# Attention stages and branch stage of a two-block fp32 layer: later output transposes, projection matmuls between transposes, and the first gates' tile moved into the last attention head

## The chip, the cores and the metric

One Trainium2 chip, one core of it. The metric is the device time of one execution in microseconds (us), the median of several runs.

## The reference, cut to what matters

Input is x of 1024 positions by 1024 channels, fp32. The first block normalises x and projects it; three branches follow (a gated linear recurrence, a differential attention of 4 heads of 2 x 64, a forgetting attention of 8 heads of 64), which are mixed by gates:

```python
h = rmsnorm(x, norm1_g); proj = h @ w_in            # q, k, v, gates, ...
o_diff = diff_attention(dq, dk, dv, lam, rel_bias)  # softmax(c=0) - lam * softmax(c=1), times v
y_diff = rmsnorm(o_diff, diff_subln_g) * (1 - lam_init)
y_fox = forgetting_attention(fq, fk, fv, log_f)
g = sigmoid(gates + gate_b)                         # three gates of 1024
m = g[0] * (y_rnn @ w_br_rnn) + g[1] * (y_diff @ w_br_diff) + g[2] * (y_fox @ w_br_fox)
x = x + m @ w_out
```

A feed-forward layer and a second block (SSD, HGRN2 and S5 mixers) follow; the change does not touch them.

## The kernel before, in words

Every fp32 matrix product is made of three fp32r matmuls: each operand is split into a high and a low part, and high x high, high x low, low x high are added in PSUM. The activations' parts are AH and AL (`act_high`, `act_low`). A weight tile of 128 columns goes through WeightTiles (line 75): SP loads it to `raw`, ACT copies it to `high` (split_high, L138), POOL makes `low` (split_low, L145), PE multiplies (multiply, L163). There are two slots; the semaphores raw_free, loaded, high, low and used count turns per slot. A whole tile is 8 x 3 x 2 = 48 matmuls of 128x512; a tile of w_br_diff or w_br_fox (NK = 4) is 24. Slots may be filled by the stage before through `Ahead` ("ready"): its tiles are split before the stage ends.

**stage_attention** runs twice, as "diff" and then as "fox". A head has 8 steps, in the order of query blocks 0, 7, 1, 6, 2, 5, 3, 4; h is the head, i the place in that order, j = 8h + i. In the program's order PE does in step j: scores(j+2) (L1332), matmuls of the projection of a later head into the bank pP (project_ahead, L1315), values(j) (L1364 for diff, L1368 for fox), more of the projection, and turned(j+1): transposes of the probabilities into the banks pT[0] and pT[1] in turn (L1351), in groups of up to four. A group may start when ACT or DVE has evacuated the group two before it. With fox both sides c = 0, 1 are transposed, so a block of 5 or more has four groups; with diff it has two. `projecting(j)` says which piece of the projection belongs to step j: 12 matmuls a step for the heads to come. In diff the last ten steps project the first head of fox (`follow`); in fox nothing is left to project there. ACT does in step j: exps(j+2), take_high(j) (fox), a take of a finished projection, evacuate(j+1), weight splits at i = 3 and i = 7. DVE does combine(j+1), reduce(j+2), take(j), evacuate(j+1).

In diff the outputs of a head must be normalised and transposed: ACT's out_root at i = 7, DVE's scale_out (L1610) writes o_scaled at i = 0 of the next head, PE's turn_out (L1377) transposes it into pT[0] and pT[1] in the same step, ACT's out_high and DVE's out_low (L1615) take it. The next transposes into these banks wait for out_low ("yl").

**stage_mix_branches** begins with the two attended branches. For each of eight chunks n and for j = 0 (diff), 1 (fox): PE multiplies the gate's tile (slot 0, 48 matmuls, pG[j]) and the branch's half tile (slot 1, 24 matmuls, pY[j]); ACT writes gate[j] = sigmoid(pG[j] + gate_b) (L625); DVE multiplies it by pY[j] (L739), adds the two (L741), and SP stores the sum. The first tile of each slot is made ahead by fox. Then follow the recurrent branch (8 pairs of whole tiles, from turn RNN_AT of the slots), its gates and its product, and w_out. SP loads the first attended tiles, then four `taps` and four `bias` rows of 4-byte elements (L445, L447), two gate tiles of the recurrence, and goes on in a loop. `over_loop` is a hardware loop with its last round written out. Each stage ends with a barrier.

Of the kernel before, what the change touches and what calls it, by code (L numbers as in the profile page):

```python
# [78 lines left out]
class WeightTiles:  # L79
# [7 lines left out]
    def __init__(self, core, ctx, sem, nk, width=P, name="w", slots=2, ready=True, place=None):  # L87
        self.sem, self.nk, self.width, self.name, self.slots = sem, nk, width, name, slots
        self.ready = ready if isinstance(ready, tuple) else (ready,) * slots
# [33 lines left out]
    def load(self, sp, slot, turn, src, nk=None):  # L123

        nk = nk or self.nk
        if self.given(slot, turn):
            return
# [4 lines left out]
    def split_high(self, act, slot, turn, nk=None):  # L132
# [3 lines left out]
        act.wait_ge(self.s("loaded", slot), (turn + (1 - self.ready[slot])) * 16)  # L136
# [192 lines left out]
def stage_mix_branches(core, X, ahead):  # L329
# [20 lines left out]
    RNN_AT = 2 * KD  # L350
# [11 lines left out]
    with stage(core) as (ctx, sem):  # L362
        W = WeightTiles(core, ctx, sem, KD)
        WR = WeightTiles(core, ctx, sem, G, HALF)
        A_next = Ahead(core, sem, ahead)
        gate_b = sbuf(core, ctx, "gate_b", [P, 3, KD])
        gate = [sbuf(core, ctx, f"gate{j}", [P, SEQ]) for j in two]
        other = [sbuf(core, ctx, f"other{j}", [P, SEQ]) for j in two]
# [33 lines left out]
        with nc.Block() as block:  # L402

            @block.sync
            def _(sp):
# [3 lines left out]
                def load_attended(n):  # L409
                    for j, (g, w, _) in enumerate(attended):  # L410
                        W.load(sp, 0, n * 2 + j, w_in[:, bass.ds(n * P + GATES_AT + g * D, P)])
                        W.load(sp, 1, n * 2 + j, w[:, bass.ds(n * P, P)], NK)

                def store(n):
                    sp.wait_ge(sem("sum"), n + 1)
                    sp.sem_inc(sem("store_asked"), 1)
                    sp.dma_start(m_tile(n), gate[0][:, :]).then_inc(sem("m_stored"), 16)
# [25 lines left out]
                load_attended(0)  # L443
# [5 lines left out]
                with sp.Fori(1, KD) as n:  # L449
                    load_attended(n)  # L450
                    store(n - 1)
# [5 lines left out]
                sp.wait_ge(sem("m_stored"), KD * 16)  # L457
# [21 lines left out]
            def _(pool):  # L479
                W.open_pool(pool)  # L480

                def attended_low(n):
                    for j in two:
                        W.split_low(pool, 0, n * 2 + j)
                        W.split_low(pool, 1, n * 2 + j, NK)
# [5 lines left out]
                first_then_loop(pool, KD, attended_low)  # L491
# [15 lines left out]
            def _(pe):  # L507
                W.open_pe(pe)
                pe.sem_inc(sem("gates_free"), 1)
                with pe.Fori(0, KD) as n:  # L510
                    for j, (_, _, y0) in enumerate(attended):
                        W.wait(pe, 0, n * 2 + j)
                        pe.wait_ge(sem(f"pg_free{j}"), n + 1)
                        W.multiply(pe, 0, pG[j], AH, AL)
                        W.wait(pe, 1, n * 2 + j)
                        pe.wait_ge(sem(f"py_free{j}"), n + 1)
                        W.multiply(pe, 1, pY[j], YH[:, y0:y0 + NK, :], YL[:, y0:y0 + NK, :], NK)

                def rnn(n, first):
                    W.wait(pe, 0, n + RNN_AT)  # L520
                    if first:
                        pe.wait_ge(sem("pg_free0"), KD + 1)
# [4 lines left out]
                    if first:  # L527
                        pe.wait_ge(sem("pg_free1"), KD + 1)
# [88 lines left out]
            def _(act):  # L617
                for j in two:
                    act.sem_inc(sem(f"pg_free{j}"), 1)  # L619
                act.wait_ge(sem("gate_b"), 48)  # L620

                def sigmoid_attended(n, j):
                    act.wait_ge(W.s("used", 0), n * 2 + j + 2)
                    act.wait_ge(sem(f"gate_free{j}"), n + 1)
                    act.activation(gate[j][:, :], flat2(pG[j]), ACT.Sigmoid, bias=gate_b[:, attended[j][0], bass.ds(n, 1)]).then_inc(sem(f"pg_free{j}"), 1)  # L625

                def attended_turn(n, more):
                    for j in two:
                        turn = n * 2 + j + 1
                        W.split_high(act, 0, turn if more or j == 0 else RNN_AT)  # L630
                        sigmoid_attended(n, j)
                        if more or j == 0:
                            W.split_high(act, 1, turn, NK)
                        else:
                            W.split_high(act, 1, RNN_AT)
# [3733 lines left out]
```

## Time and profile before

| what | us |
|---|---|
| three runs | 3072.69, 3068.14, 3072.55 |
| median | 3072.55 |
| the profiled execution, own time | 3067.96 |
| its span, first to last instruction | 3066.2 |
| diff attention, first to last matmul | 90.5 to 311 |
| fox attention, first value matmul to last value matmul | 313.2 to 568.1 |
| branch stage's first matmul | 570.4 |

Times in the rows are microseconds from the span's start. A row of the timeline gives start, duration, engine, line, operation, what it writes from what it reads, shape and count; in brackets the idle time of that engine just before, and what ended it. PE is TensorE's matmuls, DVE VectorE, ACT ScalarE, POOL GpSimd, SP the engine that issues most transfers. "issue" means that the profile shows nothing waited for. PEclk is the granted clock as a share of full speed.

### The profile page before, as it was taken

The page shows a single profiled execution, that of the slowest core. Times are in us where ns is not written, and L with a number is a line of the kernel's source. Part 1 is how long each engine was busy: PE and PEld are TensorE (multiplying, and loading weights), DVE is VectorE, ACT ScalarE, POOL GpSimd, SP SyncE. Part 2 cuts the span into 40 slices and gives each one's busy share as a digit, 9 for nine tenths or more (in the row PEclk, how much of TensorE's full clock was granted, in tenths as well). Part 3 has the DMA queues.
Part 4 walks back from the last instruction along what each step waited for, and adds up shares of the span by engine and source line. Part 5 has one row for each costly group of instructions (what it writes and reads, how often), then busy time and mean ns, then how long its engine had stood idle before and what let it go on. Part 6 is the DMA issues. An engine that isn't in the chain of part 4 may idle for free. (4 is left out here: it accounts for less than half of the span.)

```text
span 3066.2 us, 38258 instructions
## 1 busy us (share of the span) xinstructions
PE 2947.0 (96%) x14910; PEld 2389.5 (78%) x14910; DVE 1413.7 (46%) x2142; ACT 1147.5 (37%) x1587; POOL 735.0 (24%) x396
## 2 busy tenths in 40 slices
PE   8999999899999999999999999989999999999988
PEld 6777766688877788878888888877777888878776
DVE  4466244211155413344343444375553566555776
ACT  3355244322266512322222222253442554325443
POOL 2110100022211222221124421112232333123552
PEclk9999999999999999999999999999999999899988
DMA  4110200221211123131112111125323111323343
GB/s 141 44 42 8 76 28 25 41 65 56 78 47 46 53 80 117 49 88 41 41 48 62 48 48 41 41 90 103 72 87 103 42 28 35 110 43 112 119 150 110
DMA packets 250129, 203.69 MB, mean 66 GB/s; under 512 B 38453, under 2 KB 219141, under 8 KB 249997
## 3 DMA queue, kind: packets, MB, share of 16 engines
q1 hardware_dynamic: 247820, 200.84, 22.5%
q8 instruction: 88, 1.44, 0.2%
q10 hardware_dynamic: 2176, 1.05, 0.2%
q14 instruction: 45, 0.36, 0.0%
HBM read 174.69 MB, written 27.16 MB: 66 GB/s over the span
## 5 line engine op out<-in xcount | busy, mean ns | idle before, releaser
L145 POOL TENSOR_TENSOR w_low<-w_raw,w_high 128x1024 fp32r<-128x1024 f32 (+1 forms) x181 | 418.7, 2313 | 1704.8 <-ACT w_high L138 1701.5
L138 ACT ACTIVATE w_high<-w_raw 128x1024 fp32r<-128x1024 f32 (+1 forms) x181 | 180.9, 1000 | 417.1 <-PE mix_banks L163 292.0
L163 PE MATMUL ffn_banks<-act_high,w_high 128*128 128x512 f32 x688 | 268.8, 391 | 4.0 <-POOLq L112 4.0
L163 PE MATMUL ffn_banks<-act_high,w_low 128*128 128x512 f32 x688 | 268.4, 390 | 0.0
L163 PE MATMUL ffn_banks<-act_low,w_high 128*128 128x512 f32 x688 | 268.4, 390 | 0.0
L163 PE MATMUL mix_banks<-act_high,w_high 128*128 128x512 f32 x640 | 252.3, 394 | 2.3 <-POOLq L112 2.3
L163 PE MATMUL mix_banks<-act_high,w_low 128*128 128x512 f32 x640 | 249.1, 389 | 0.0
L163 PE MATMUL mix_banks<-act_low,w_high 128*128 128x512 f32 x640 | 249.0, 389 | 0.0
L163 PEld LDWEIGHTS ffn_banks<-act_high,w_high 128*128 128x128 f32 x688 | 129.7, 189 | 31.2 <-POOLq L112 4.3
L2063 DVE TENSOR_TENSOR x<-x,ffn_banks 128x512 f32<-128x512 f32 x176 | 117.8, 685 | 73.9 <-PE ffn_banks L1829 73.4
L163 PEld LDWEIGHTS ffn_banks<-act_high,w_low 128*128 128x128 f32 x688 | 129.6, 188 | 27.0
L163 PEld LDWEIGHTS ffn_banks<-act_low,w_high 128*128 128x128 f32 x688 | 129.6, 188 | 26.9
L1829 PE MATMUL ffn_banks<-v_high,f_high 128*128 128x512 f32 x352 | 140.8, 400 | 9.6 <-DVE x L2063 9.4
L1948 ACT ACTIVATE u_val<-ffn_banks,conv 128x1024 f32<-128x1024 f32 x21 | 25.3, 1207 | 321.4 <-PE ffn_banks L163 321.4
L163 PEld LDWEIGHTS mix_banks<-act_high,w_high 128*128 128x128 f32 x640 | 120.1, 188 | 29.0 <-ACTq L619 2.5
L163 PEld LDWEIGHTS mix_banks<-act_low,w_high 128*128 128x128 f32 x640 | 120.1, 188 | 26.7 <-issue 1.9
L163 PEld LDWEIGHTS mix_banks<-act_high,w_low 128*128 128x128 f32 x640 | 120.1, 188 | 25.0
L1829 PE MATMUL ffn_banks<-v_high,f_low 128*128 128x512 f32 x352 | 139.4, 396 | 0.0
L1829 PE MATMUL ffn_banks<-v_low,f_high 128*128 128x512 f32 x352 | 137.7, 391 | 0.0
L1442 ACT ACTIVATE scores<-scores,low 128x1024 f32<-128x1024 f32 (+7 forms) x128 | 98.4, 770 | 100.7 <-DVE low L1552 100.6
L739 DVE TENSOR_TENSOR gate<-gate,mix_banks 128x1024 f32<-128x1024 f32 x16 | 19.5, 1221 | 231.3 <-PE mix_banks L163 231.3
L2071 DVE SCALAR_TENSOR_TENSOR u_val<-ffn_banks,conv,u_val 128x1023 f32<-128x1023 f32 x21 | 26.9, 1283 | 198.5 <-ACT u_val L1948 198.5
(660 smaller groups left out, 7000.6 us busy)
## 6 DMA issues: line engine op xcount, KB each, us to landing
w_raw<-in_w_in SPq DMA_DIRECT2D x106, 512.0 KB, 4.1
w_raw<-in_ffn_up SPq DMA_DIRECT2D x44, 512.0 KB, 3.9
w_raw<-in_w_out SPq DMA_DIRECT2D x24, 512.0 KB, 3.8
v_raw<-in_ffn_down SPq DMA_DIRECT2D x11, 1024.0 KB, 5.1
decay<-acum_rows SPq DMA_DIRECT2D x16, 512.0 KB, 3.7
exp_c<-exp_acum_rows SPq DMA_DIRECT2D x16, 512.0 KB, 5.2
x_ring<-in_x SPq DMA_DIRECT2D x8, 512.0 KB, 9.8
m_part<-gate SPq DMA_DIRECT2D x8, 512.0 KB
```

Source lines behind the costliest of these rows:

```text
L138: act.activation(self.high[slot][:, 0:nk, :], self.raw[slot][:, 0:nk, :], ACT.Copy).then_inc(self.s("high", slot), 1)
L145: pool.tensor_tensor(self.low[slot][:, 0:nk, :], self.raw[slot][:, 0:nk, :], self.high[slot][:, 0:nk, :].bitcast(F32), ALU.subtract).then_ ...
L163: last = pe.matmul(out[:, h, :] if not halves else out[h], w[slot][:, k, :], x[:, k, cols], start=(n == 0), stop=(n == 3 * nk - 1))
L739: dve.tensor_tensor(gate[j][:, :], gate[j][:, :], flat2(pY[j]), ALU.mult).then_inc(sem(f"py_free{j}"), 1)
L1442: act.activation(tile, tile, ACT.Exp, scale=-1.0, bias=low[:, b, c:c + 1], accum_out=total[:, b, c:c + 1]).then_inc(sem("probs"), 1)
L1829: last = pe.matmul(pD[:, bank_of(i, q), :], x[:, k, steps(b)], w[0][:, k, half * HALF:(half + 1) * HALF], start=(n == 0), stop=(n == 3 * G ...
L1948: act.activation(U[:, :], flat2(pU[slot]), ACT.Identity, scale=taps[:, 2, bass.ds(n, 1)], bias=bias[:, bass.ds(n, 1)]).then_inc(sem(f"tap2 ...
L2063: dve.tensor_tensor(X[:, b, cols], X[:, b, cols], pD[:, bank_of(i, q), :], ALU.add).then_inc(sem("added"), 1)
L2071: dve.scalar_tensor_tensor(out=U[:, 1:], in0=x[:, :SEQ - 1], scalar=taps[:, 1, bass.ds(n, 1)], in1=U[:, 1:], op0=ALU.mult, op1=ALU.add).th ...
```

## The change

Three parts. (1) In diff, turn_out, out_high and out_low move from step i = 0 to i = 1 of the next head, with the wait on "yl" and the split of the step's projection. (2) Where a step has projection matmuls left after values(j) and the next block has four groups of transposes, they are issued between its second and its third group. (3) Fox's last ten steps project two gate tiles (`follow` = the first tiles of gates 1 and 2) in pieces of 6 x 12 and 4 x 6 matmuls into first_q and first_k, which the branch stage takes as gate[0] and gate[1] and passes through a sigmoid in place. The branch stage's attended loop then runs half tile, gate tile of the next chunk, half tile, gate tile: all half tiles in slot 0 but the very last, gate tiles in slot 1; two gate tiles fewer. Slot 1 is handed over loaded but not split ("raw"). The sum goes to other[0]. SP's tap, bias and recurrence loads come ahead of the loop's.

```diff
 class WeightTiles / __init__
+        states = ready if isinstance(ready, tuple) else (ready,) * slots
+        self.ready = [state is True for state in states]
+        self.loaded = [state in (True, "raw") for state in states]
 stage_mix_branches
-    RNN_AT = 2 * KD
+    RNN_AT = 2 * KD - 1
+        W = WeightTiles(core, ctx, sem, KD, ready=(True, "raw"))
+        gate = [core.first_q, core.first_k]
 ... sync
+                def load_attended(n, more):
+                    W.load(sp, 0, n * 2 + 1, y_tile(n, 1), NK)
+                    W.load(sp, 1, n * 2 + 1, g_tile(n + 1, 1))
+                    W.load(sp, 0, n * 2 + 2, y_tile(n + 1, 0), NK)
+                    if more:
+                        W.load(sp, 1, n * 2 + 2, g_tile(n + 2, 0))
+                    else:
+                        W.load(sp, 1, n * 2 + 2, y_tile(n + 1, 1), NK)
-                load_attended(0)
                 for j in range(4):
                     sp.dma_start(taps[:, j, :], per_channel(io["rnn_conv_w"][0, j])).then_inc(sem("small"), 16)
...
+                def attended_turn(n, more):
+                    load_attended(n, more)
+                    store(n)
+                over_loop(sp, KD - 1, attended_turn)
 ... tensor
+                with pe.Fori(0, KD - 1) as n:
+                    for j in two:
+                        attended_y(n, j, 0, n * 2 + j)
+                        W.wait(pe, 1, n * 2 + j)
                         pe.wait_ge(sem(f"pg_free{j}"), n + 1)
-                        W.multiply(pe, 0, pG[j], AH, AL)
+                        W.multiply(pe, 1, pG[j], AH, AL)
+                for j in two:
+                    attended_y(KD - 1, j, j, 2 * KD - 2)
 ... scalar
+                def sigmoid_attended(n, j):
+                    act.wait_ge(W.s("used", 1), n * 2 + j)
+                    act.wait_ge(sem("sum"), n)
+                    act.activation(gate[j][:, :], flat2(pG[j]), ACT.Sigmoid, ...).then_inc(sem(f"pg_free{j}"), 1)
+                def attended_turn(n, more):
+                    W.split_high(act, 0, n * 2 + 1, NK)
+                    W.split_high(act, 1, n * 2 + 1)
+                    W.split_high(act, 0, n * 2 + 2, NK)
+                    sigmoid_attended(n + 1, 0)
+                    W.split_high(act, 1, n * 2 + 2, None if more else NK)
+                    sigmoid_attended(n + 1, 1)
+                W.split_high(act, 1, 0)
+                act.wait_ge(sem("gate_b"), 48)
                 for j in two:
+                    act.activation(gate[j][:, :], gate[j][:, :], ACT.Sigmoid, ...).then_inc(sem(f"pg_free{j}"), 1)
 ... vector
                     dve.wait_ge(sem("m_stored"), (n + 1) * 16)
+                    dve.tensor_tensor(other[0][:, :], gate[0][:, :], gate[1][:, :], ALU.add).then_inc(sem("sum"), 1)
 stage_attention
-    last_head = NH if diff else NH - 1
+    last_head = NH
+    last_counts = (12, 12, 12, 12, 8, 8, 8, 8, 8, 8) if diff else (12,) * 6 + (6,) * 4
 ... turned
+                    for at, (N, n, c, g, count) in enumerate(own_groups(j)):
+                        if between and at == 2:
+                            project_ahead(*between)
...
-                        if diff and i == 1 and h and n < ends[0, 0] + 2:
+                        if diff and h and ends[1, 0] <= n < ends[1, 0] + 2:
                             pe.wait_ge(sem("yl"), 2 * (h - 1) + n % 2 + 1)
 ... steps on PE
-                        before = 0 if j == last_step else 4 if i == 0 and h else 8
+                        before = 0 if diff and j == last_step else 4 if diff and i == 1 and h else min(8, count)
...
-                    if diff and i == 0 and h:
+                    if diff and i == 1 and h:
                         turn_out(h - 1)
-                    if ahead_now and count > before:
-                        project_ahead(H, g, first + before, count - before)
+                    rest = (H, g, first + before, count - before) if ahead_now and count > before else None
+                    inside = rest and j < last_step and len(own_groups(j + 1)) > 2
+                    if rest and not inside:
+                        project_ahead(*rest)
                     if j < last_step:
-                        turned(j + 1)
+                        turned(j + 1, rest if inside else None)
 first_block
+        stage_attention(core, "fox", FQ, FK, FV, 4, [(0, w_diff[:, 0:P]), (1, gate(1)[:, P:2 * P])], follow=(GATES_AT + D, GATES_AT + 2 * D))
```

ACT's out_high and DVE's out_low get the same condition `i == 1`. At its end fox's ACT waits until the raw tile has landed.

## Rows read from the trace of the kernel before

**Rows 1.** Page: busy time, share of the span and instructions of each engine.

```profile
PE 2947.0 (96%) x14910; PEld 2389.5 (78%) x14910; DVE 1413.7 (46%) x2142; ACT 1147.5 (37%) x1587; POOL 735.0 (24%) x396
```

**Rows 2.** Windows: busy (count) of PE, PEld, DVE, ACT, POOL; PEclk, DMA share, GB/s.

```profile
464.26:519.28 55.02, 53.18 (x378) 37.30 (x377) 26.00 (x88) 26.59 (x63) 4.79 (x2) 1.00 0.07 22
519.28:561.80 42.52, 32.16 (x281) 20.98 (x280) 25.19 (x84) 21.57 (x56) 1.39 (x1) 0.96 0.01 1
570.40:698.00 127.60, 127.58 (x563) 105.65 (x564) 14.21 (x10) 31.66 (x31) 26.83 (x15) 1.00 0.28 63
```

**Rows 3.** PE's waits, total, times, longest: two within diff, one over the span.

```profile
PE pt L1377 <- DVE o_scaled L1610: 6.3, 4, 1.9
PE pt L1351 <- DVE y_low L1615: 2.0, 2, 1.0
...
PE pt L1351 <- issue: 13.0, 16, 2.8
```

**Rows 4.** Timeline of PE in diff: three steps with output transposes.

```profile
167.53 0.70 PE L1332 MATMUL ps<-k,q 64*128 64x256 f32 x4
...
171.45 1.09 PE L1377 MATMUL pt<-ident,o_scaled 128*128 128x128 f32 x8 [1.86 <-DVE o_scaled L1610]
...
176.42 1.77 PE L1332 MATMUL ps<-k,q 64*128 64x512 f32 x8
...
216.78 0.70 PE L1332 MATMUL ps<-first_k,first_q 64*128 64x256 f32 x4
...
226.06 1.77 PE L1332 MATMUL ps<-first_k,first_q 64*128 64x512 f32 x8
...
309.11 1.09 PE L1377 MATMUL pt<-ident,o_scaled 128*128 128x128 f32 x8 [0.79 <-DVE o_scaled L1610]
```

**Rows 5.** Chain that ended last: start, us, what (two 48-matmul tiles in a row).

```profile
2710.29 22.02 PE ssd_banks L163 x96
```

**Rows 6.** Windows again, columns as in rows 2, around the second head's transposes.

```profile
220.00:224.00 4.00, 3.30 (x12) 3.01 (x13) 3.76 (x7) 3.62 (x8) 2.69 (x1) 0.60 0.00 0
```

**Rows 7.** Lines of PE from 519.28 us on (busy, mean, idle before), then its timeline.

```profile
L1351 PE MATMUL pt<-ident,scores 128*128 128x128 f32 x83 | 12.6, 287 | 8.4 <-issue 8.1 <-DVE scores L1579 0.3
L1368 PE MATMUL po<-probs_t,v_fox 128*64 128x128 f32 x180 | 12.0, 278 | 3.6 <-ACT probs_t L1452 3.4
...
534.32 1.53 PE L1351 MATMUL pt<-ident,scores 128*128 128x128 f32 x8 [2.75 <-issue]
...
563.08 1.09 PE L1368 MATMUL po<-probs_t,v_fox 128*64 128x128 f32 x16 [1.28 <-ACT probs_t L1452]
...
566.80 1.31 PE L1368 MATMUL po<-probs_t,v_fox 128*64 128x128 f32 x20 [0.58 <-ACT probs_t L1452]
```

**Rows 8.** Timeline of SP, ACT, POOL and DVE at the branch stage's start.

```profile
569.58 1.62 SPq L407 DMA_DIRECT2D gate_b<-in_gate_b  x3
...
576.68 1.28 ACT L138 ACT_TABLE_LOAD   x1 [8.22 <-DMA w_raw<-in_w_in]
581.63 1.06 ACT L138 ACTIVATE w_high<-w_raw 128x1024 fp32r<-128x1024 f32 x1 [3.67 <-PE mix_banks L163]
...
584.00 1.12 ACT L625 ACTIVATE gate<-mix_banks,gate_b 128x1024 f32<-128x1024 f32 x1
...
582.77 2.40 POOL L145 TENSOR_TENSOR w_low<-w_raw,w_high 128x1024 fp32r<-128x1024 f32 x1 [51.22 <-ACT w_high L138]
...
604.65 1.88 DVE L741 TENSOR_TENSOR gate<-gate,gate 128x1024 f32<-128x1024 f32 x1
```

**Rows 9.** SP's tap loads; a window (as rows 2); transfers' KB and us to landing.

```profile
572.55 5.25 SPq L445 DMA_DIRECT2D taps<-in_rnn_conv_w  x4
...
571.00:572.00 1.00, 1.00 (x6) 0.82 (x5) 0.00 (x0) 0.00 (x0) 0.00 (x0) 1.00 0.79 6
...
w_raw<-in_w_br_fox SPq DMA_DIRECT2D x1, 256.0 KB, 5.6
w_raw<-in_w_br_diff SPq DMA_DIRECT2D x1, 256.0 KB, 2.8
```

More of the change, by code:

```diff
@@ L125, in load @@
         nk = nk or self.nk
-        if self.given(slot, turn):
+        if self.loaded[slot] and isinstance(turn, int) and turn == 0:
             return
@@ L135, in split_high @@
             return
-        act.wait_ge(self.s("loaded", slot), (turn + (1 - self.ready[slot])) * 16)
+        if not (self.loaded[slot] and isinstance(turn, int) and turn == 0):
+            act.wait_ge(self.s("loaded", slot), (turn + (1 - self.loaded[slot])) * 16)
         act.wait_ge(self.s("used", slot), turn + 1)
@@ L362, in stage_mix_branches @@
     with stage(core) as (ctx, sem):
-        W = WeightTiles(core, ctx, sem, KD)
-        WR = WeightTiles(core, ctx, sem, G, HALF)
+        W = WeightTiles(core, ctx, sem, KD, ready=(True, "raw"))
+        WR = WeightTiles(core, ctx, sem, G, HALF, ready=(True, "raw"))
         A_next = Ahead(core, sem, ahead)
+        other = [sbuf(core, ctx, "other0", [P, SEQ])]
+        sbuf(core, ctx, "gate_place", [P, 2, SEQ])
+        gate = [core.first_q, core.first_k]
+        other.append(sbuf(core, ctx, "other1", [P, SEQ]))
         gate_b = sbuf(core, ctx, "gate_b", [P, 3, KD])
-        gate = [sbuf(core, ctx, f"gate{j}", [P, SEQ]) for j in two]
-        other = [sbuf(core, ctx, f"other{j}", [P, SEQ]) for j in two]
         taps = sbuf(core, ctx, "taps", [P, 4, KD])
@@ L416, in store @@
                     sp.sem_inc(sem("store_asked"), 1)
-                    sp.dma_start(m_tile(n), gate[0][:, :]).then_inc(sem("m_stored"), 16)
+                    sp.dma_start(m_tile(n), other[0][:, :]).then_inc(sem("m_stored"), 16)
                 def load_rnn(n):
@@ L480, in _, with attended_low @@
                 W.open_pool(pool)
[L482 to L485, printed above, removed]
+                def attended_low(n, more):
+                    W.split_low(pool, 0, n * 2 + 1, NK)
+                    W.split_low(pool, 1, n * 2 + 1)
+                    W.split_low(pool, 0, n * 2 + 2, NK)
+                    W.split_low(pool, 1, n * 2 + 2, None if more else NK)
                 def rnn_low(n):
@@ L1124, in _, with stage_attention @@
                 dve.tensor_tensor_scan(c[:, :], f[:, :], z[:, :], 0.0, ALU.mult, ALU.add).then_inc(sem("c"), 1)
-def stage_attention(core, kind, q_at, k_at, v_at, y0, ahead, follow=None):
+def stage_attention(core, kind, q_at, k_at, v_at, y0, ahead, follow):
     nc, io = core.nc, core.io
@@ L1169, in projecting @@
         return NH, done // (3 * KD), done % (3 * KD), last_counts[n]
-    head_columns = lambda slot, h: (follow or (q_at, k_at))[slot] if h == NH else (q_at, k_at)[slot] + h * P
+    head_columns = lambda slot, h: follow[slot] if h == NH else (q_at, k_at)[slot] + h * P
     with stage(core) as (ctx, sem):
@@ L1433, in take_projection @@
                     act.activation((Q, K)[slot][H % 2][:, half * HALF:(half + 1) * HALF], source, ACT.Copy,
-                                   scale=0.125 * -1.0 if slot == 0 else 1.0).then_inc(sem("qk"), 1)
+                                   scale=0.125 * -1.0 if slot == 0 and (diff or H < NH) else 1.0).then_inc(sem("qk"), 1)
                 def exps(j):
@@ L1472, in split_tile @@
                         W.split_high(act, slot, h + T0)
-                    elif h == last_head + 1:
+                    elif h == last_head + 1 and slot == 0:
                         nxt.split_high(act, slot)
@@ L1630, in _ @@
                     take(j)
-                    if diff and i == 0 and h:
+                    if diff and i == 1 and h:
                         out_low(h - 1)
```

79 lines of the change are left out of this document (30 added, 49 removed).

## The prediction, made before the changed kernel ran

> **What bounds the kernel now.** I read the page first: TensorE is busy for 96% of the span [rows 1]. So a change pays only where it takes work off PE or fills time in which PE waits. Next I read the stretches. In the branch stage PE is busy for 127.58 of 127.60 us at full clock: a matmul less there is a matmul less of time [rows 2]. In forgetting attention (kind "fox") eight steps with projections run ahead take 55.02 us and hold 53.18 us of PE. The same eight steps of the last head, which has nothing to project, take 42.52 us and hold only 32.16 us, at a mean granted clock of 0.96 [rows 2]. That head is where time lies idle.
>
> PE's waits in differential attention show what the first edit is after: 6.3 us on o_scaled in four waits, 2.0 us on y_low in two [rows 3]. In time order, with scores of one step to scores of the next as the ruler, the step that turns the outputs round takes 8.89 us (167.53 to 176.42) and holds a wait of 1.86 us on o_scaled and one of 1.0 us on y_low (one of the two of [rows 3]). The next head's takes 9.28 us (216.78 to 226.06) [rows 4].
>
> **The change, part by part.** A long matmul costs 22.02 us per 96 in a row, 0.23 us each [rows 5]; a weight tile of 48 is 11.0 us, a half tile (NK = 4) of 24 is 5.5 us.
>
> *Late output transposes.* Three of the four o_scaled waits fall at step 0 of a head. The fourth closes the stage at 309 us and stays (0.79 us) [rows 4]. With turn_out one step later, o_scaled (ready when the transposes start at 171.45) is early by the transposes, scores and values that then stand before them, some 5 us: 6.3 - 0.8 = 5.5 us. The two y_low waits, 2.0 us, go as well: the transposes of the block with one group now follow eight fillers (1.9 us), and ACT, no longer held by the table loads around the root, takes out_t at once. I leave 0.5 us for a rest of it. The second head's step was slower although it had no y_low wait: 9.28 - (8.89 - 1.0) = 1.4 us, in which the granted clock was 0.60 over 4 us [rows 6], between the levels 1.2 and 2.4 GHz. Before it fell PE had stood waiting for o_scaled. Without that wait I take it as gone too. Nothing is added but order; the stage's four-filler cover moves from step 0 to step 1. Sum: -5.5 - 2.0 - 1.4 + 0.5 = **-8.4 us**, bounds -9 (all goes) and -4 (the waits shift to the bigger step, the clock dip stays).
>
> *Filler between transposes.* PE waited 13.0 us in 16 places before the second pair of transposes (the releaser is "issue", it is ACT's evacuation of the first pair's bank) [rows 3]. Of this 8.1 us is in the stretch from 519.28 on, where no filler exists [rows 7]. The other eleven waits sum to 4.9 us, 0.45 each. Four fillers, 0.93 us, now stand there; they came from just before the first pair, whose operands are ready: even in the last head, where nothing stands before the first pair, PE waits for DVE's combine only 0.3 us in all [rows 7]. So the waits go whole: **-4.9 us**, bounds -5 and -2 (if switching between matmul kinds costs a quarter us each).
>
> *The gates' first tile in fox's last head.* 96 matmuls, 22.0 us, enter the last ten steps: six pieces of 12, four of 6. For all eight steps with 12 the two stretches of rows 2 give the answer directly: 55.02 - 42.52 = 12.5 us for 96 matmuls. Here four waits of about 0.45 are hidden by the edit above, less one in a step that gets no inner filler: -1.3. The last two of those steps get 6 instead of 12: -12 x 0.23 = -2.8. The last two steps of the stage get 12 together, +2.8, and hide PE's waits for ACT of 1.28 and 0.58 us [rows 7]: +0.9. Sum +9.3 us. Check: PE's waits there are 8.4 + 3.6 = 12.0 us [rows 7], and a mean clock of 0.96 over 42.52 us, where a wait of 2.75 us stood [rows 2, 7], cost about 1.7; 22.0 - 12.0 - 1.7 = +8.3 if all is filled, which is the lower bound. Upper bound: nothing hides, +22.0. I take **+9.3**, since it comes from measured steps of the same shape. ACT's last evacuation, 0.6 us, ends after DVE's last take (0.29): the barrier comes 0.3 us later. The weight splits and loads of the new tiles take the places of those made ahead (slot 1's split grows from a half tile to a whole one, 1.06 us on ACT and 2.40 on POOL [rows 8], and is due three steps later): nothing.
>
> *The branch stage* loses two tiles of 48: **-22.0 us**, as PE has no idle to absorb it [rows 2]. What may be given back:
> The start. PE does the half tile (5.5 us) and then wants the raw tile's split and both halves of `gate` done. Split: table load 1.28, ACT 1.06, POOL 2.40 [rows 8] from about 569.6: ready near 574.5, wanted at 575.9. The in-place sigmoids wait for gate_b, three small loads issued at 569.58 [rows 8]. I saw no landing, only bounds: ACT had passed its wait by 576.68, and rows for a 1 us stretch in which only such loads run show the queue busy but moving 6 GB/s, so 12 KB take 2 us [rows 9]. With landing at 573, a 1.28 us load of the table and 1.12 of sigmoid [rows 8] it is 575.5 to 576: stall 0.3 us; with landing at 576.7 it is 3.2 us. I take 0.3, by the stretch.
> The second half tile's load is moved past eight tap and bias loads and two rnn gate loads on SP's queue. The four tap loads took 5.25 us to issue behind two tiles; gate_b's three, with nothing ahead, took 0.54 us each [rows 8, 9]. At 0.6 the ten are out by 577.5, so the half tile is issued near 578 and lands 2.8 us later [rows 9]. Then 1.28 for the table load at the head of ACT's loop and halves of 1.06 and 2.40 (0.6 and 1.3): ready at 584.2; PE wants it at 586.9. If nothing is gained by the new order (taps 5.25, the rest 6 x 0.6: issued at 580.5, landing 5.6) it is 589.4: 2.6 us. I take 0, by the row with nothing ahead.
> Steady state. A gate tile in slot 1 is split while PE does a half tile: 581.4 to 585.2, 3.8 of 5.5 us, as now with slot 0 [rows 8]. sigmoid (n+1, 0) waits for `sum`, two passes of DVE of at most 1.88 us [rows 8], about 3.2 us after the half tile's end; ACT must split again 10.95 us after that end. Stores leave from other[0], which is rewritten 33 us later. DMAs: the same bytes, two tiles earlier. Nothing.
> Net **-21.7 us**, bounds -22 and -16.2.
>
> One rule speaks against this part. The trace shows a table load of 1.28 us, and 1.31 us between the end of ACT's first split (582.69) and its first sigmoid (584.00), with such a load between [rows 8]. The Trainium skill, ScalarE: Activation LUTs, What ACT_TABLE_LOAD costs, adds a drain of about 1.38 us, 2.66 us in all for a switch. By it the start would stall 1.7 us instead of 0.3, and the sum be 1.4 less; the row decides.
>
> **Sum**: -8.4 - 4.9 + 9.3 + 0.3 - 21.7 = -25.4 us. The profiled execution took 3067.96 us (span 3066.2); so 3042.6. The median shown, 3072.55, is 4.6 higher, and the three runs fall at 3068 and 3072.6 with nothing between; I forecast **3045**, the middle of 3042.6 and 3047.2. A measurement of this kernel tells 0.2% (6 us) from no change.
>
> **Rivals.**
> A, *the filler hides nothing* (chance 0.12): the last head is ruled by the chain DVE combine, reduce, ACT exp, evacuate, and every inserted matmul delays its head. For it: PE waited 8.1 us on exactly that chain, 2.75 us once [rows 7]. Against: with 12 fillers in, the same waits were 0.45 us each. It gives -8.4 - 4.9 + 22.0 + 0.3 - 21.7 = -12.7: 3055 to 3060.
> B, *the start of the branch stage stalls* (0.08): both bounds above are met, 3.2 and 2.6 us in place of 0.3: 3042.6 + 5.5 = 3048 to 3053.
> C, *slower* (0.03): the new chain in the gates' loop, one store old, decides: PE's tile, DVE product and sum, ACT sigmoid, then ACT's split of the next gate tile behind it. It is free until `sum` is late by 10.95 - 3.2 - 2.4 (sigmoid and table load) = 5.35 us plus PE's spare 1.7, 7 us. Seven turns must then lose 31 us together to end 0.2% slower: sum 11.5 us late, for instance behind a store that lands so late. At 12 us late: 3042.6 + 7 x 5 = 3078. Against: DMA is at 0.28 of its share there [rows 2].
> D, *the waits in diff only move* (0.05), with the rest as forecast: 3047 to 3050. The forecast itself has 0.72.
>
> **Numbers.** Range 3038 to 3058: below, all bounds of gain, -9 - 5 + 8.3 + 0.3 - 22 = -27.4 from 3067.96, and a little; above, A. Outside it lie C and a part of A. Faster by over 0.2%: 0.95 (forecast, A, B, D less a bit); same 0.03; slower 0.02.
>
> **What would show it.** Branch stage: PE without a wait, its first 48-matmul gate tile after a 24-matmul one, and 22 us shorter. Diff: no wait of PE on o_scaled but the last, step 0 near 6 us. Fox: waits before the second pair gone in three heads; last head some 9 us longer with full clock. I am wrong if PE waits in the last head still sum to over 5 us, if the waits reappear on y_low or probs_t, or if gate_b or a late half tile holds PE for more than 1 us at the stage's start.

## The result, and the profile after

| | before | changed |
|---|---|---|
| median of four runs, us | 3071.27 | 3048.31 |
| lowest to highest | 3068.14 to 3072.69 | 3042.59 to 3049.26 |
| ratio, 95% interval | | 0.9923 [0.9911, 0.9935] |
| profiled execution | 3067.96 | 3048.71 |

23.0 us less in the medians, 19.3 in the two profiled executions. The forecast, 3045, is 3.3 us too low, and the range held it. The page of the changed kernel shows the same PE work in a shorter span.

```profile
span 3047.0 us, 38217 instructions
...
PE 2947.0 (97%) x14910; PEld 2391.0 (78%) x14910; DVE 1410.7 (46%) x2142; ACT 1134.5 (37%) x1578; POOL 732.7 (24%) x396
```

The times at which PE begins its stages, read from the first matmul of each line, say where the time came from. Lengths are in us; in brackets, where it is not nothing, stands the time for which the profile's clock was at its lower level, 1.2 GHz ("the low clock" from here on).

| stretch of PE | before | changed | difference |
|---|---|---|---|
| start to first scores of diff | 114.0 (3.4) | 114.4 (3.4) | +0.4 |
| diff, to fox's first value matmul (L1309, 306.69) | 199.17 (3.6) | 192.30 | -6.9 |
| fox's value projection | 45.23 (3.2) | 45.34 (3.4) | +0.1 |
| fox, three heads, to the fourth's first scores (504.77) | 160.83 | 152.74 | -8.1 |
| last head and barrier, to the branch stage's first matmul (564.31) | 51.15 (3.4) | 59.54 | +8.4 |
| branch stage to the first w_out matmul (1179.58) | 637.03 | 615.27 | -21.8 |
| **lead there** | | | **-27.9** |
| all the rest, to the last matmul; no line of it was touched | 1846.20 (88.7) | 1855.52 (99.0) | +9.3 |

So by the end of what the change touches it leads by more than I forecast (25.4), and then a third of the lead is lost in code that is the same in both. The pair overstates this loss: the profiled execution of the kernel before (3067.96 us) is 3.3 us quicker than its median, that of the changed kernel 0.4 us slower.

PE's waits of the changed kernel, as in [rows 3] (line, releaser, total, times, longest), first within diff, then from the first scores of fox to the branch stage:

```profile
PE pt L1375 <- DVE y_low L1643: 2.8, 3, 1.0
PE pt L1401 <- DVE o_scaled L1638: 0.8, 1, 0.8
...
PE mix_banks L166 <- POOLq L114: 2.5, 1, 2.5
PE pt L1375 <- issue: 1.1, 2, 0.6
PE pp L1337 <- issue: 0.2, 1, 0.2
```

The o_scaled waits have gone but the last (0.8). In their place stand three waits on y_low, 2.8 us, where two stood with 2.0. Of fox's 13.0 us before the second pair of transposes 1.1 are left, both in the last head, and its 3.4 us for probs_t have gone.

Windows of the changed kernel (columns as in [rows 2]): last head, start of the branch stage, untouched code; then the untouched code of the kernel before.

```profile
504.77:564.31 59.54, 55.94 (x423) 40.02 (x423) 27.18 (x92) 29.36 (x69) 3.66 (x2) 1.00 0.04 10
564.30:698.00 133.70, 133.69 (x590) 110.74 (x591) 16.71 (x12) 26.05 (x28) 31.14 (x17) 1.00 0.28 66
1179.58:3035.10 1855.52, 1793.30 (x9103) 1491.07 (x9101) 939.36 (x1147) 660.30 (x849) 530.07 (x293) 0.97 0.24 72
```

```profile
1207.46:3053.66 1846.20, 1786.85 (x9103) 1486.35 (x9101) 939.71 (x1147) 660.30 (x849) 532.25 (x293) 0.98 0.25 72
```

In the last head PE is busy for 55.9 of 59.5 us at full clock. From its first matmul on, PE has no wait in this window (133.69 of 133.70), and the profile shows none in the rest of the branch stage either.

**The branch stage's start**, against [rows 8] and [rows 9], on SP, ACT, POOL and PE:

```profile
563.46 1.61 SPq L412 DMA_DIRECT2D gate_b<-in_gate_b  x3
565.12 3.55 SPq L455 DMA_DIRECT2D taps<-in_rnn_conv_w  x4
...
572.46 0.43 SPq L437 DMA_DIRECT2D wi<-in_rg_w_i  x1
573.32 0.41 SPq L132 DMA_DIRECT2D w_raw<-in_w_br_fox  x1
...
563.79 1.06 ACT L141 ACTIVATE w_high<-w_raw 128x1024 fp32r<-128x1024 f32 x1 [1.10 <-PEq L123]
564.87 1.28 ACT L655 ACT_TABLE_LOAD   x1
567.26 1.15 ACT L655 ACTIVATE first_q<-first_q,gate_b 128x1024 f32<-128x1024 f32 x1 [1.11 <-DMA gate_b<-in_gate_b]
568.32 1.14 ACT L655 ACTIVATE first_k<-first_k,gate_b 128x1024 f32<-128x1024 f32 x1
576.41 0.63 ACT L141 ACTIVATE w_high<-w_raw 128x512 fp32r<-128x512 f32 x1 [6.95 <-DMA w_raw<-in_w_br_fox]
581.02 1.06 ACT L141 ACTIVATE w_high<-w_raw 128x1024 fp32r<-128x1024 f32 x1 [3.98 <-PE mix_banks L166]
...
564.93 2.40 POOL L148 TENSOR_TENSOR w_low<-w_raw,w_high 128x1024 fp32r<-128x1024 f32 x1 [18.65 <-ACT w_high L141]
577.12 1.28 POOL L148 TENSOR_TENSOR w_low<-w_raw,w_high 128x512 fp32r<-128x512 f32 x1 [9.79 <-ACT w_high L141]
...
564.31 0.49 PE L166 MATMUL mix_banks<-y_high,w_high 128*128 128x512 f32 x1 [2.46 <-POOLq L114]
...
569.87 0.39 PE L166 MATMUL mix_banks<-act_high,w_high 128*128 128x512 f32 x1
```

The margins can be read here. gate_b, issued at 563.46, released ACT at 567.26: 3.8 us, where I had put 3.4. The first sigmoid ends at 568.41, PE wants its bank at 569.87: 1.5 us to spare, where my sum gave a stall of 0.3. The table load (564.87 to 566.15) was over before gate_b landed, and I had set it behind the landing. By the Trainium skill (ScalarE: Activation LUTs, What ACT_TABLE_LOAD costs) another 1.38 us of drain would have ended at 567.53, 0.27 us after the sigmoid is shown to begin; the transfer hides nearly all of such a drain, so this row neither needs it nor disproves much of it. Other rows do speak against it: in both kernels the shortest time from the end of one ACTIVATE to the start of the next with a table load between them is 1.31 us, which leaves 0.03 us beside the load's 1.28. The half tile was issued 9.0 us after the stage's first matmul (573.3), where I had put 7.6: the four tap loads took 3.55 us to issue, between the 2.4 that I took and the 5.25 of before. It landed by 576.4, and its low part was done at 578.4; PE takes it at 580.8. No second table load stands in that chain, which gives back most of the delay.

### The profile page after: what moved, and what is told of

The parts are those of the page before. It is cut to its first block and busy times, and to the rows that moved or that the text cites. A ratio compares the mean times of both kernels' runs of the same rounds, so it can differ in the third digit from the quotient of the medians.

```text
span 3047.0 us, 38217 instructions
## 1 busy us (share of the span) xinstructions
PE 2947.0 (97%) x14910; PEld 2391.0 (78%) x14910; DVE 1410.7 (46%) x2142; ACT 1134.5 (37%) x1578; POOL 732.7 (24%) x396
## 5 line engine op out<-in xcount | busy, mean ns | idle before, releaser
L166 PE MATMUL mix_banks<-act_high,w_high 128*128 128x512 f32 x608 | 239.8, 394 | 0.0
L166 PE MATMUL mix_banks<-act_high,w_low 128*128 128x512 f32 x608 | 236.7, 389 | 0.0
L166 PE MATMUL mix_banks<-act_low,w_high 128*128 128x512 f32 x608 | 236.6, 389 | 0.0
L166 PEld LDWEIGHTS mix_banks<-act_high,w_high 128*128 128x128 f32 x608 | 114.2, 188 | 25.4 <-issue 1.9
L1337 PE MATMUL pp<-act_high,w_high 128*128 128x512 f32 x256 | 106.6, 416 | 0.2 <-issue 0.2
```

The costliest lines, as they stand in the source:

```text
L166: last = pe.matmul(out[:, h, :] if not halves else out[h], w[slot][:, k, :], x[:, k, cols], start=(n == 0), stop=(n == 3 * nk - 1))
L1337: last = pe.matmul(pP[:, :], w[slot][:, k, :], x[:, k, half * HALF:(half + 1) * HALF], start=(n == 0), stop=(n == 3 * KD - 1))
```

## Experiments

All lengths are between the same starts as in the table above. Where only one execution was profiled, its total has no interval, and the stretches carry the reading. Six profiles hold the same code up to the end of the branch stage (the changed kernel three times, and three with only fills behind that stage). In them diff took 192.22 to 192.30 us, fox's three heads 152.74 to 152.75 and its last head 59.52 to 59.54. The stretches beside them move with the low clock: fox's value projection 45.1 us (3.0) to 46.5 (5.8), the branch stage 615.3 (0) to 616.7 (3.1). The start up to the first scores took 113.1 to 114.4 us, always with 3.4. So a stretch may be compared to 0.1 us at like clock, but the time at the end of the branch stage only to some 2 us.

**One part at a time.** First only the output transposes, on the kernel before:

```diff
-                        before = 0 if j == last_step else 4 if i == 0 and h else 8
+                        before = 0 if j == last_step else 4 if i == 1 and h else 8
-                    if diff and i == 0 and h:
+                    if diff and i == 1 and h:
                         turn_out(h - 1)
```

(and the same for out_high, out_low and the wait on yl)

> Only the output transposes of differential attention are moved to step 1 of the next head. My theory: the three waits on o_scaled (5.5 us) go, three new waits of 0.9 us on y_low stand in their place, and the second head's clock dip goes, so that the first matmul of forgetting attention comes 6 to 7 us earlier than in the kernel before and everything up to the branch stage's last product keeps just that lead. The rival, that the waits move whole to the bigger step, gives 3 us or less. In the code that no part of the change touches (all after the branch stage) I expect the lead to drift by some microseconds either way with the granted clock, and not because of the edit.

Measured: diff 192.28 us, -6.9, as expected; fox's first three heads 160.75, as before. The last head took 51.67, 0.5 us more than before, with 6.8 us at the low clock in place of 3.4. From the first scores to the first w_out matmul 6.4 us are left of the 6.9. The waits of PE:

```profile
PE pt L1351 <- DVE y_low L1615: 2.8, 3, 1.0
...
PE pt L1377 <- DVE o_scaled L1610: 0.8, 1, 0.8
```

The three new waits are the edit's own. The work of ACT and DVE on the first head's outputs, in the second head of the changed kernel, shows why (PE, then ACT and DVE):

```profile
167.94 0.70 PE L1354 MATMUL ps<-k,q 64*128 64x256 f32 x4
...
171.68 1.03 PE L1375 MATMUL pt<-ident,scores 128*128 128x128 f32 x8
172.65 1.77 PE L1354 MATMUL ps<-k,q 64*128 64x512 f32 x8
...
175.38 1.95 PE L1388 MATMUL po<-v_diff,probs_t 128*128 128x128 f32 x16
177.17 1.04 PE L1401 MATMUL pt<-ident,o_scaled 128*128 128x128 f32 x8
...
181.02 0.41 PE L1375 MATMUL pt<-ident,scores 128*128 128x128 f32 x2 [0.97 <-DVE y_low L1643]
```

```profile
177.74 1.03 ACT L1468 ACTIVATE scores<-scores,low 128x896 f32<-128x896 f32 x1
...
178.76 1.24 ACT L1494 ACTIVATE y_high<-pt,gain 128x512 fp32r<-128x512 f32 x2
...
179.46 1.41 DVE L1643 SCALAR_TENSOR_TENSOR y_low<-pt,gain,y_high 128x512 fp32r<-128x512 f32 x2 [1.19 <-ACT y_high L1494]
```

PE has the outputs transposed from 177.17 on, but ACT is in its second exp until 178.76, so y_high comes 1.6 us after the transposes began, and PE, through with its eight fillers, stands 0.97 us for y_low. The two steps together (from the scores of 64x256 on) took 13.42 us in each of the three heads, where they had taken 15.56, 15.98 and 15.56 before.

Second, only the filler between the transposes, on the kernel before:

```diff
+                        if between and at == 2:
+                            project_ahead(*between)
...
+                    inside = rest and j < last_step and len(own_groups(j + 1)) > 2
+                    if rest and not inside:
+                        project_ahead(*rest)
-                        turned(j + 1)
+                        turned(j + 1, rest if inside else None)
```

> Only the filler between the transposes. In the kernel before the eleven waits that it can cover are shown as 4.9 us; with the whole change the stretch became 8.1 us shorter. Theory 1: a wait shown between two transposes is short of what it costs, since the shown end of a transpose (0.27 us) is later than the time at which PE could have begun the next (0.11 us), so the edit alone gives 8 us as well, 0.7 us per wait, all before the last head begins. Rival: only 4.9 us is its, and the other 3 us came from elsewhere in the change; then this run shows 5 us.

Measured: 152.71 us for the three heads, -8.1. So the whole 8.1 us is this edit's, for eleven waits shown as 4.9. (In this execution the other stretches up to the first w_out matmul were longer than before by 4.0 us together, with 27.3 us at the low clock in place of 10.2, so that only 4.1 us of lead are left there, counted from the first scores.) The same step (blocks 2 and 6 of the third head) before, PE's timeline:

```profile
494.36 0.66 PE L1368 MATMUL po<-probs_t,v_fox 128*64 128x128 f32 x8
494.95 0.50 PE L1315 MATMUL pp<-act_high,w_low 128*128 128x512 f32 x1
...
496.00 0.93 PE L1351 MATMUL pt<-ident,scores 128*128 128x128 f32 x7
497.33 0.96 PE L1351 MATMUL pt<-ident,scores 128*128 128x128 f32 x7 [0.41 <-issue]
498.21 1.56 PE L1332 MATMUL ps<-first_k,first_q 64*128 64x512 f32 x8
```

and in the changed kernel:

```profile
481.26 0.66 PE L1392 MATMUL po<-probs_t,v_fox 128*64 128x128 f32 x8
481.85 0.99 PE L1375 MATMUL pt<-ident,scores 128*128 128x128 f32 x7
482.60 0.48 PE L1337 MATMUL pp<-act_high,w_low 128*128 128x512 f32 x1
...
483.61 0.93 PE L1375 MATMUL pt<-ident,scores 128*128 128x128 f32 x7
484.46 1.56 PE L1354 MATMUL ps<-first_k,first_q 64*128 64x512 f32 x8
```

From the start of the first seven transposes to what follows them it is 1.33 us before and 0.75 after: 0.58 us of PE were free, while the wait is shown as 0.41. A wait is counted from the shown end of the transpose before it, and that end lies one duration (0.27) after its start, when the next transpose could have begun after 0.11. The whole step is 0.65 us shorter (from the values to the scores: 3.85 and 3.20); the last 0.07 may be the switch between the matmuls of values and the long ones (the first long one behind values takes 0.50, behind transposes 0.48, the others 0.39).

Third, the change without this filler:

```diff
-                    inside = rest and j < last_step and len(own_groups(j + 1)) > 2
+                    inside = False
```

> The whole change without the filler between the transposes (it stands before the first pair again, also in the last head). Theory 1: up to the last head it is 8.1 us later than the changed kernel, and in the last head some 2 us more (three steps with 12 matmuls and an inner place, 0.7 us each). The last head then takes 61 to 62 us to the branch stage's first matmul, against 59.5 with the whole change and 51.1 without any projection in it. If instead the inner place is what lets the last head absorb its projection, it loses more than 4 us.

Measured: 160.72 us for the three heads and 61.79 for the last head, both as expected. The last head absorbs its projection without the inner place too.

Fourth, two of the four matmuls between the pairs and two before the first:

```diff
+                    if inside and rest[3] > 2:
+                        project_ahead(*rest[:3], rest[3] - 2)
+                        rest = (*rest[:2], rest[2] + rest[3] - 2, 2)
```

> The whole change, but only two of the four matmuls stand between the two pairs of transposes, and the other two before the first pair. The runs so far: none between gives 160.7 us for the first three heads of forgetting attention, four give 152.7 us. If a wait costs what is shown (0.30, 0.41, 0.51, 0.62 us), two matmuls (0.54 us) cover all but one, and the three heads take 153 us. If each costs some 0.25 us more than shown, as theory 1 has it (0.55 to 0.87 us), two matmuls leave 0 to 0.35 us of it in each place, 0.6 us per head: 154 to 155 us.

Measured: 155.71 us, beyond both expectations: two matmuls take 5.0 of the 8.0 us. The same step shows the gap directly:

```profile
484.90 0.93 PE L1375 MATMUL pt<-ident,scores 128*128 128x128 f32 x7
485.58 0.47 PE L1337 MATMUL pp<-act_low,w_high 128*128 128x512 f32 x1
485.89 0.40 PE L1337 MATMUL pp<-act_high,w_low 128*128 128x512 f32 x1
486.23 0.95 PE L1375 MATMUL pt<-ident,scores 128*128 128x128 f32 x7
```

From the first seven transposes to the second it is 1.33 us (484.90 to 486.23), as in the kernel before with nothing between (496.00 to 497.33): two matmuls, some 0.54 us of PE, went in without moving what follows, in a wait shown as 0.41. So the direction is theory 1's. What it missed is probably the switch: a first long matmul behind values is followed after 0.34 us, the others after 0.23, and with two before the first pair this comes back in all eleven places. Eleven times 0.11 is 1.2 us, an estimate, and 155.7 less 1.2 is within its 154 to 155. No run tests the switch alone.

**The last head.** The gates' tile in eight pieces of 12:

```diff
-    last_counts = ... else (12,) * 6 + (6,) * 4
+    last_counts = ... else (12,) * 8 + (0,) * 2
```

> The gates' first tile in eight pieces of 12, so that the last two steps of forgetting attention have none. By my steps, steps 4 and 5 get 12 matmuls more (2.8 us), of which the inner place in step 4 hides 0.75, and the last two steps lose 2.8 us of matmuls but get back their waits for ACT's evacuation, 1.28 and 0.58 us and 0.2 to 0.3 of drain: the last head takes 59.5 + 2.05 - 0.7 = 60.9 us instead of 59.5. If those two waits were only a shadow of DVE's chain, it takes 59.5 or less.

Measured: 60.25 us. Fewer than 60.9, more than 59.54: matmuls in the last two steps do hide waits, but the gain over this order is 0.7 us and not 1.4. PE's waits from 504 us on:

```profile
PE po L1392 <- ACT probs_t L1478: 1.4, 2, 0.8
PE pt L1375 <- issue: 0.6, 1, 0.6
```

The wait for probs_t is 1.4 in place of the 1.28 + 0.58 that I had put back; that the 12 matmuls in step 5 took the rest is likely, and not shown.

**Two more edits.** In diff the second half of the outputs goes first, as the next transposes want its bank; in steps 4 and 6 of the last head two of six matmuls go between the pairs:

```diff
-                    for g in range(2):
+                    for g in (1, 0):
...
-                            pe.wait_ge(sem("yl"), 2 * (h - 1) + n % 2 + 1)
+                            pe.wait_ge(sem("yl"), 2 * (h - 1) + 2 - n % 2)
...
-... else min(8, count)
+... else 4 if count == 6 and i % 2 == 0 else min(8, count)
```

(and the same order in out_high and out_low)

> The whole change with two more: in differential attention the second half of the outputs is transposed and taken first, since the next transposes want that bank; and in the last head of forgetting attention two of the six matmuls of steps 4 and 6 stand between the pairs of transposes. I expect the three new waits on y_low to fall from 0.9 to 0.2 us each (differential attention 190.1 us instead of 192.3) and the last head to lose 1 us of its 59.5. Against: in step 6 four matmuls may not cover the wait of values for ACT's evacuation, and the last head stays at 59 us or more.

Measured: diff 190.27, last head 58.64, both as expected. Its waits on these lines:

```profile
PE pt L1375 <- DVE y_low L1643: 0.9, 3, 0.3
...
PE pt L1375 <- issue: 0.2, 1, 0.2
```

Then both timed on one chip:

> The kernel with the swapped output halves and the inner place for the pieces of six, timed. Up to the end of the branch stage it was 2.9 us ahead of the changed kernel in its look (differential attention 190.3 against 192.3 us, last head 58.6 against 59.5). Against the changed kernel timed on the same chip I expect 2 to 4 us less in the median, 3044 to 3047 us, with single runs of both spread over 6 us or more by the clock in the later code.

> The changed kernel, timed again on the same chip as its neighbour. If the loss in the later code were the program's, its runs would lie within 2 us of 3048. If it is dealt by the clock, they spread from about 3042 to 3050 us, and the mean lead over the kernel before is nearer to 22 to 24 us than to the 27.9 us that it has where the branch stage ends.

Measured: 3044.43 us (3042.63 to 3046.87), ratio to the kernel before 0.991 [0.9895, 0.9925]; the changed kernel 3048.27 (3045.0 to 3050.28), 0.9922 [0.9909, 0.9936]. The changed kernel's runs don't all lie within 2 us of 3048, and its median leads the kernel before's (3071.9 over nine runs) by 23.6 us, as expected.

The new version is ahead by 3.8 us in the medians, but the intervals overlap, and the stretches don't carry the claim. The expectation says that it led by 2.9 us up to the end of the branch stage. That is the sum of the two stretches that the edits touch. Over all stretches from the first scores to the first w_out matmul it took 1064.6 us in its first profile, against 1065.2 of the changed kernel. In the two timed ones, the new version's and the changed kernel's (sums of five windows, columns as in [rows 2] without clock and DMA):

```profile
sum 1065.05, PE 1056.90 PEld 825.12 DVE 423.56 ACT 429.46 POOL 181.57; mean PE 211.38 PEld 165.02 DVE 84.71 ACT 85.89 POOL 36.31
```

```profile
sum 1065.11, PE 1054.15 PEld 823.52 DVE 423.65 ACT 429.41 POOL 181.64; mean PE 210.83 PEld 164.70 DVE 84.73 ACT 85.88 POOL 36.33
```

Diff and the last head are 2.0 and 0.9 us shorter in both profiles of the new version. In both, fox's value projection is 0.7 and 1.2 us longer (5.0 and 5.9 us at the low clock, not 3.4) and the branch stage 1.6 us longer (3.4, not 0). Two fills behind the branch stage gave a profile with both lengthenings (1.1 and 1.4 us) and the changed kernel's own code ahead of them, so they can come without the edits. Whether the edits bring them on is open, and that the new version is faster is not shown.

**Where a third of the lead went.** The changed kernel again, untouched:

> The changed kernel again, not a letter changed. Of the 27.9 us that it led with at the end of the branch stage's last product, 9.0 us were lost in code that is the same in both kernels. Theory: this is the granted clock, which falls in the stages with short work and waits at places that differ from execution to execution. Then the same program shows in this run the same times up to the branch stage's end within 0.5 us, and another length of the rest, by up to 6 us, with another number of microseconds at the low clock. Rival: the loss belongs to the program (where its code and its transfers lie); then the rest takes the same time again within 1 us, at the same places.

Measured: up to the branch stage's end all within 0.1 us, as expected. The rest took 1854.3 us, against 1855.5, and 1855.4 in the profile of the timed run above: not the free spread that I expected, much nearer to the rival. Within it the two executions did part: the second had its low clock at other places behind 2640 us, was 3.5 us ahead at one point (a group of matmuls that starts at 2914.96 in the first starts at 2911.49 there) and 1.3 at the end. Then useless fills behind the branch stage, in front of the same code:

```diff
                 A_next.split_low(pool)
+                pool.wait_ge(sem("low"), NB)
+                for spare in (squares,):            # two and three buffers in the next runs
+                    pool.memset(spare[:, :], 0.0)
```

> The changed kernel with a useless fill of one 128x1024 buffer on GpSimd at the end of the branch stage, so that all the code behind it starts about 1 us later. From the first matmul with w_out to the last matmul the kernel before took 1846.2 us with 88.7 us at the low clock, the changed kernel 1855.5 and 1854.3 us with 99.0 and 95.6. Theory: it is where the falls of the clock meet the short-work stretches of this code that costs the 9 us, and any shift of a microsecond or two deals it anew: less the fill's own time, the stretch comes out anywhere from 1845 to 1856 us. Rival: the loss belongs to the changed program, then it stays at 1854 to 1856 us plus the fill.

> The same with two fills, so about 2 us later than the changed kernel. Theory and rival as for one fill: anywhere from 1845 to 1856 us less the fills, and another value than with one fill, or 1854 to 1856 us with both. The stretch in which the second block's heads are turned (184.4 us with no low clock, 185.9 with 3.4 us of it, 188.2 with 6.8) should again go by its low clock alone.

> The changed kernel with three fills on GpSimd before the feed-forward stage. One fill gave 1850.5 us from the first w_out matmul to the last matmul (its own time, 0.5 us, in it), two gave 1858.5 (2.0 in it), none 1855.5 and 1854.3. The theory (clock) says that a third gives yet another value between 1845 and 1856 us less the fills; the rival, that the delay itself is what counts, says about 1860.

| kernel | untouched code, us | at the low clock | one stretch of it (before: 2216 to 2401) |
|---|---|---|---|
| before | 1846.2 | 88.7 | 184.4 (0) |
| only late outputs | 1849.7 | 95.6 | 185.9 (3.4) |
| only filler | 1849.6 | 95.6 | 187.8 (6.8) |
| eight twelves | 1848.3 | 88.7 | 187.1 (3.4) |
| no filler between | 1853.9 | 95.6 | 188.3 (6.8) |
| two between | 1850.8 | 95.6 | 186.6 (3.4) |
| two more edits | 1850.7 | 92.2 | 185.6 (0) |
| two more edits, timed run | 1851.5 | 99.0 | 188.3 (6.8) |
| changed | 1855.5 | 99.0 | 188.2 (6.8) |
| changed, again | 1854.3 | 95.6 | 188.3 (6.8) |
| changed, timed run | 1855.4 | 99.0 | 188.3 (6.8) |
| changed, one fill | 1850.5 | 92.2 | 186.9 (3.4) |
| changed, two fills | 1858.5 | 102.4 | 188.3 (6.8) |
| changed, three fills | 1854.3 | 99.0 | 186.5 (3.4) |

One fill made this code 3.8 to 5.1 us faster than it is in the three executions of the changed kernel, fill included. The eight-twelves kernel, with the same code behind and one number changed far ahead of it, took 6.0 to 7.2 us less. Three fills fit the theory as well (1854.3, where the delay alone would give some 1860). Two do not: less the fills it is 1856.5, just outside the theory's 1845 to 1856 and at the rival's. The one stretch goes mostly by its low clock, but not by that alone as I expected: 184.4 and 185.6 us with none, 185.9 to 187.1 with 3.4.

So the loss isn't fixed to what the changed kernel does in this code. It goes with the time at the low clock, but not by its amount alone: half of 10.3 us is 5.2, and 9.3 were lost. By the windows above PE was busy for 6.45 us more over the same 9103 matmuls, and waited 2.9 us more. Where a low stretch lies counts too. One place shows it, in the same turn of a loop. A wait of 4.05 us for DVE ends at 2158.38 before and at 2132.23 in the changed kernel. The low stretch of 6.83 us began 2.2 us ahead of that end before, and 0.9 us behind it in the changed kernel. Windows over the low stretch alone, before and changed:

```profile
2156.19:2163.02 6.83, 4.55 (x34) 3.78 (x35) 6.45 (x15) 0.00 (x0) 0.72 (x1) 0.50 0.01 2
```

```profile
2133.10:2139.93 6.83, 5.95 (x30) 4.56 (x26) 6.41 (x14) 0.00 (x0) 0.00 (x0) 0.50 0.00 0
```

Before, 2.2 us of the low clock fell on waiting. In the changed kernel it reached 3.7 us into the long matmuls behind the group, against 0.7: from the first of them to the tenth it is 3.88 us instead of 2.49. From some 2010 to 2200 us 20.5 us are at the low clock in either kernel, and the changed one took 2.4 us longer.

What stays open is the other half of the rival, that each program has a value of its own, by where its code and transfers lie. The three executions of the changed kernel lie within 1.2 us and the two of the kernel with two more edits within 0.8, while different kernels are up to 12.3 us apart. The other kernels, the one before among them, were profiled once. Against it stands only that the changed kernel's nine timed runs spread over 7.7 us and those of the kernel before, timed with it, over 9.5 (3066.77 to 3076.3).

## Why the prediction was right, point by point

*Late output transposes*: forecast -8.4, measured -6.9, confirmed alone. The waits on o_scaled went but the last, and the second head's clock dip with them (no low clock in diff). The step that failed is "I leave 0.5 us for a rest of it": it rested on "ACT ... takes out_t at once". ACT had the next block's exps in hand, and three waits of 0.93 us on y_low stand there, 2.8 us. With 2.8 in place of 0.5 the sum would be -6.1; the three heads gained some 0.2 us each beyond the waits shown. The sign "step 0 near 6 us" was off too: it took 4.7 us, as the output transposes had left it together with the waits, and the step behind it 8.7 instead of 6.7.

*Filler between transposes*: forecast -4.9, measured -8.1, beyond my bound of -5. The failed step is "the other eleven waits sum to 4.9 us, 0.45 each": I took shown waits for lost time. In the step looked at they cost 0.58 where 0.41 is shown. The bound of -2, for switches between kinds of matmul, had no ground in a row, and no run shows such a loss.

*The last head*: forecast +9.3 and 0.3 for the barrier, measured +8.4. Steps of one shape with and without the filler, read off the same trace, gave the size; the sum over waits gave +8.3. But that check is near for a wrong reason. It put 1.7 us on the clock dip, while the late-outputs run, with 3.4 us more at the low clock in this head, took 0.5 us more. And of the 22.0 us put in, 13.6 are hidden, where the waits shown fell by 10.9 (12.0 to 1.1). Here too the waits hid more than was shown.

*The branch stage*: forecast -21.7, measured -21.8. There was no stall at its start: the slack was 1.5 us, where my sum had a stall of 0.3, and 2.4 us, where it had a slack of 2.7. This part never ran alone; its number is read from the stretch.

*Sum*: -25.4 forecast, -27.9 measured where the touched code ends. That is beyond the sum of all my bounds of gain (-27.4), by the filler's. The misses have opposite signs: +1.5, -3.2, -1.2 and -0.1, and +0.5 in stretches that I left out. I counted nothing behind it, and that was the largest miss: +9.3 in the profiled pair, some 5 in the medians (27.9 - 23.0).

*Rivals*: A fell (of the 22.0 us put into the last head 8.4 are paid, where A had all of them). B and C fell: PE has no wait in the branch stage. D was in part right: where 7.5 us of waits were to go, 2.8 stand on y_low. That the forecast 3045 came near 3048.3 owes something to misses that cancel.

## What to carry to other kernels

Filler of known length, put exactly into the gap between two dependent groups, was worth more here than the waits that the profile shows (8.1 us for 4.9), and two steps of one shape in the same trace, one with and one without it, price it best. Before moving work behind another engine's queue, ask what that engine does at the new place: the wait follows the queue. And measure such a change stretch by stretch, with the low clock of each beside it: the rest of a long kernel can take back or give some microseconds, and so can the stretches next to an edit. A sum of only those stretches that an edit touches is not its lead.

## What the runs showed of the hardware that I had not expected

In the step looked at, the wait shown behind short matmuls understates the free time by about a matmul's duration less its spacing (0.41 shown, 0.58 gained; 0.27 and 0.11 us), and two matmuls of some 0.54 us together fit in without moving what follows. Identical code of 1850 us took from 1846.2 to 1858.5 us over the 14 profiles of this study, with 88.7 to 102.4 us at the low clock, and one fill more ahead of it shortened it by 3.8 to 5.1.
